# The experts' down products as three fp32r ones, with weight parts by half units

## The reference, cut to what matters

```
hid = silu(einsum('td,edf->etf', t, w_gate)) * einsum('td,edf->etf', t, w_up)   # 1024 -> 512
hid = hid * combine.T[:, :, None]        # two experts of sixteen for each token
y = einsum('etf,efd->td', hid, w_down)   # 512 -> 1024
```

## Time and profile before

| | us |
|---|---|
| median of 3 runs | 2130.91 |
| lowest and highest | 2128.61, 2133.64 |
| the profiled execution | 2131.86 |
| its span (first to last instruction) | 2130.3 |
| the experts' rounds in it, from the first slot rows asked for to the last down's end | 588.1 to 951.9 |

### The profile page before, as it was taken

How to read it: one execution, slowest core, us unless ns; L and a number is a source line. 1 busy time by engine, 2 the same in 40 slices (tenths; PEclk the granted TensorE clock), 3 DMA queues, 4 the chain that set the end, 5 groups by cost and what they waited for, 6 DMA issues and landing times.

```text
span 2130.3 us, 22099 instructions
## 1 busy us (share of the span) xinstructions
PE 1841.3 (86%) x8371; PEld 1407.6 (66%) x8371; DVE 849.6 (40%) x1337; ACT 775.0 (36%) x1222; POOL 280.7 (13%) x380
## 2 busy tenths in 40 slices
PE   5995999999469998975999999697777859999996
PEld 4883666668346666644888888585463648888885
DVE  3545334434435555545332332623443262323324
ACT  3224554542234444433222222322546232213221
POOL 2100432220100000001000000513406100000000
PEclk9997999999689999996999999897779879999998
DMA  5226523124369999674332332323010022323321
GB/s 179 87 82 216 197 76 116 57 83 168 150 231 341 345 337 343 226 248 154 93 98 89 110 91 87 102 89 104 1 40 1 30 70 79 99 89 99 99 99 50
DMA packets 182126, 279.69 MB, mean 131 GB/s; under 512 B 9554, under 2 KB 135073, under 8 KB 169616
## 3 DMA queue, kind: packets, MB, share of 16 engines
q1 hardware_dynamic: 170000, 244.36, 34.8%
q0 software_dynamic: 12032, 34.06, 4.7%
HBM read 241.13 MB, written 35.16 MB: 130 GB/s over the span
## 4 chain that ended last, share of the span: by engine, by line
PE 78%; DVE 8%; DMA 5%; ACT 3%; issue 3%; POOL 2%; SPq 0%; POOLq 0%; DVEq 0%; ACTq 0%
PE psum L402 21%; PE psum L403 20%; PE psum L404 20%; PE psum L1143 5%; PE psum L538 3%; PE psum L556 3%; PE psum L527 2%; DMA arena<-x_slots 2%; DVE warea_r L373 2%; POOL arena L645 2%; DMA warea<-in_w_in 1%; ACT warea_r L366 1%; DVE tarea_r L1655 1%; PE psum L1112 1%; DVE harea L1627 1%
## 5 line engine op out<-in xcount | busy, mean ns | idle before, releaser
L393 DVE TENSOR_TENSOR warea_r<-warea,warea_r 128x2048 fp32r<-128x2048 f32 x114 | 266.6, 2339 | 411.2 <-ACT warea_r L387 411.1
L402 PE MATMUL psum<-tarea_r,warea_r 128*128 128x512 f32 x896 | 357.4, 399 | 12.6 <-DVE tarea_r L1655 12.6
L403 PE MATMUL psum<-tarea_r,warea_r 128*128 128x512 f32 x896 | 351.9, 393 | 0.0
L404 PE MATMUL psum<-tarea_r,warea_r 128*128 128x512 f32 x896 | 351.5, 392 | 0.0
L387 ACT ACTIVATE warea_r<-warea 128x2048 fp32r<-128x2048 f32 x114 | 217.7, 1911 | 289.7 <-PE psum L404 281.3
L402 PE MATMUL psum<-warea_r,arena_r 128*128 128x512 f32 (+1 forms) x640 | 251.2, 392 | 34.5 <-DVE warea_r L373 31.0
L404 PE MATMUL psum<-warea_r,arena_r 128*128 128x512 f32 (+1 forms) x640 | 247.0, 386 | 0.0
L403 PE MATMUL psum<-warea_r,arena_r 128*128 128x512 f32 (+1 forms) x640 | 246.8, 386 | 0.0
L402 PEld LDWEIGHTS psum<-tarea_r,warea_r 128*128 128x128 f32 x896 | 170.1, 190 | 53.6 <-DVE tarea_r L1655 13.3
L404 PEld LDWEIGHTS psum<-tarea_r,warea_r 128*128 128x128 f32 x896 | 170.1, 190 | 36.3
L403 PEld LDWEIGHTS psum<-tarea_r,warea_r 128*128 128x128 f32 x896 | 170.2, 190 | 33.6
(11 more groups left out here) (290 smaller groups left out, 2405.7 us busy)
## 6 DMA issues: line engine op xcount, KB each, us to landing
warea<-in_ffn_w_gu SPq DMA_DIRECT2D x88, 512.0 KB, 5.0
warea<-in_w_in SPq DMA_DIRECT2D x48, 512.0 KB, 4.7
warea<-in_ffn_w_down SPq DMA_DIRECT2D x40, 512.0 KB, 4.2
arena<-in_w_up SPq DMA_DIRECT2D x16, 1024.0 KB, 6.5
tarea<-in_w_up SPq DMA_DIRECT2D x16, 1024.0 KB, 6.8
tarea<-in_w_down SPq DMA_DIRECT2D x16, 1024.0 KB, 5.6
warea<-in_w_gate SPq DMA_DIRECT2D x14, 1024.0 KB, 8.8
harea<-in_w_gate SPq DMA_DIRECT2D x14, 1024.0 KB, 8.2
```

The costliest lines, as they stand in the source:

```text
L393: dve.tensor_tensor(w_lo[:, u % 2, :], raw[:, u % RAW, :], w_hi[:, u % 2, :].bitcast(f32), ALU.subtract)\
L402: nc.tensor.matmul(out, high, by_high, start=first, stop=False)
L403: nc.tensor.matmul(out, high, by_low, start=False, stop=False)
L404: return nc.tensor.matmul(out, low, by_high, start=False, stop=last)
```

## The change

- The hidden features are split in `HT_hi` (ScalarE) and `HT_lo` (VectorE), and a down product is three fp32r ones, which read `w_hi` and `w_lo`. So the down units go through `moe_high` and `moe_low` as well, in the order of the units.
- A part is made, waited for and released by halves of a unit, 1024 columns: `moe_hi`, `moe_lo` and `moe_done` count halves.
- A place of the ring of raw weights is free when its low part exists (`moe_lo`), no longer when its matmuls are through.
- The queues of ScalarE and VectorE get the down units' parts: ScalarE after the silu, VectorE partly before `hb` and partly after it. `HT_lo` stands before `y_copy`.
- Before the last down, TensorE reads no register any more.

The diff, cut to its core:

```diff
-    HTs = carve(5120, 4, P)
+    HT_hi, HT_lo = part(A_AT + 5120, 4, P), part(A_AT + 5632, 4, P)
...
     def moe_high(b, i):
...
         act.wait_ge(moe_in[slot], 16 * fills)
-        if i >= 2:
-            act.wait_ge(s["moe_done"], n - 1)
-        elif not isinstance(b, int) or b >= 1:
-            act.wait_ge(s["moe_done"], n - 3 if not isinstance(b, int) or b >= 2 else i + 3)
-        act.activation(w_hi[:, parity, :], moe_raw[slot], ACT.Copy).then_inc(s["moe_hi"], 1)
+        for h in range(2):
+            at = ds(1024 * h, 1024)
+            if not (isinstance(n, int) and n < 2):
+                act.wait_ge(s["moe_done"], 2 * (n - 2) + (h + 1))
+            act.activation(w_hi[:, parity, at], moe_raw[slot][:, at], ACT.Copy).then_inc(s["moe_hi"], 1)
 
     def moe_low(b, i):
...
-        dve.wait_ge(s["moe_hi"], 4 * b + (i + 1))
-        dve.tensor_tensor(w_lo[:, parity, :], moe_raw[slot], w_hi[:, parity, :].bitcast(f32), ALU.subtract)\
-            .then_inc(s["moe_lo"], 1)
+        for h in range(2):
+            at = ds(1024 * h, 1024)
+            dve.wait_ge(s["moe_hi"], 2 * n + (h + 1))
+            dve.tensor_tensor(w_lo[:, parity, at], moe_raw[slot][:, at], w_hi[:, parity, at].bitcast(f32), ALU.subtract)\
+                .then_inc(s["moe_lo"], 1)
...
                 if isinstance(n, int) and n >= 12 and b < STATIC:
-                    sp.wait_ge(s["moe_done"], n - 11)
+                    sp.wait_ge(s["moe_lo"], 2 * (n - 11))
                 elif not isinstance(n, int):
-                    sp.wait_ge(s["moe_done"], n - 5)
+                    sp.wait_ge(s["moe_lo"], 2 * (n - 5))
...
             def gate_up(b):
                 pe.wait_ge(s["xt_low"], 2 * b + 2)
                 for i in range(4):
-                    pe.wait_ge(s["moe_lo"], 4 * b + (i + 1))
+                    n = moe_unit(b, i)[0]
                     for k in range(4):
-                        c = 4 * (i % 2) + k
+                        c, h = 4 * (i % 2) + k, k // 2
+                        if k % 2 == 0:
+                            pe.wait_ge(s["moe_lo"], 2 * n + (h + 1))
...
-                    mm.then_inc(s["moe_done"], 1)
+                        if k % 2:
+                            mm.then_inc(s["moe_done"], 1)
...
-                pe.wait_ge(s["hts_ready"], b + 1)
+                pe.wait_ge(s["hts_low"], b + 1)
...
                 for i in range(2):
-                    n, slot, fills = moe_unit(b + 1, first_unit + i)
-                    pe.wait_ge(moe_in[slot], 16 * (filled if filled is not None else fills))
+                    n = moe_unit(b + 1, first_unit + i)[0]
                     for c in (2 * i, 2 * i + 1):
+                        pe.wait_ge(s["moe_lo"], 2 * n + (c % 2 + 1))
                         for hf in range(2):
                             at = 1024 * (c % 2) + 512 * hf
-                            mm = nc.tensor.matmul(ps[4 + hf], HTs[:, c, :], moe_raw[slot][:, at:at + 512], start=c == 0, stop=c == 3)
-                    mm.then_inc(s["moe_done"], 1)
+                            mm = products(ps[4 + hf], HT_hi[:, c, :], HT_lo[:, c, :], w_hi[:, i % 2, at:at + 512],
+                                          w_lo[:, i % 2, at:at + 512], c == 0, c == 3)
+                        mm.then_inc(s["moe_done"], 1)
...
                 nc.scalar.activation(sg, ps[0], ACT.Silu).then_inc(s["silu_done"], 1)
+                if not zero:
+                    moe_high(b, 4)
+                    moe_high(b, 5)
                 slot_high(b + 1)
-                for i in range(2):
-                    moe_high(b + 1, i)
+                moe_high(b, 4 if zero else 6)
+                moe_high(b, 5 if zero else 7)
                 act.wait_ge(s["htr_psum"], b + 1)
-                nc.scalar.activation(HTs, ps[6].rearrange("p (c q) -> p c q", c=4), ACT.Copy).then_inc(s["hts_ready"], 1)
+                nc.scalar.activation(HT_hi, ps[6].rearrange("p (c q) -> p c q", c=4), ACT.Copy).then_inc(s["hts_ready"], 1)
...
-                for i in (2, 3):
+                for i in (2, 3, 4):
                     moe_low(b, i)
                 dve.wait_ge(s["silu_done"], b + 1)
-                dve.wait_ge(s["moe_done"], n0 + 4)
+                dve.wait_ge(s["moe_done"], 2 * n0 + 8)
                 V.tensor_tensor(hb, ps[1], sg, ALU.mult).then_inc(s["hb_ready"], 1)
+                if not zero:
+                    moe_low(b, 5)
                 slot_low(b + 1)
-                for i in range(2):
-                    moe_low(b + 1, i)
                 if not zero:
-                    y_copy(b - 1, n0 + 6)
+                    moe_low(b, 6)
+                moe_low(b, 5 if zero else 7)
+                dve.wait_ge(s["hts_ready"], b + 1)
+                V.tensor_tensor(HT_lo, ps[6].rearrange("p (c q) -> p c q", c=4), HT_hi.bitcast(f32), ALU.subtract)\
+                    .then_inc(s["hts_low"], 1)
+                if not zero:
+                    y_copy(b - 1, 2 * n0 + 12)
```

More of the change, by code:

```diff
@@ L330, in build_blocks @@
         route_psum chosen exp_in exp_out slots_ready routed zero_ready zero_out scattered x_slot xtr_psum xt_ready xt_low
-        silu_done hb_ready htr_psum hts_ready yb_ready yb_high y_out y_back0 y_back1 y_back2 y_back3 y_used
+        silu_done hb_ready htr_psum hts_ready hts_low yb_ready yb_high y_out y_back0 y_back1 y_back2 y_back3 y_used
         ff_silu gated hid_high ff_hid fd_psum f_evac
@@ L768, in _ @@
                 n, slot, _ = moe_unit(last + 1, i)
-                sp.wait_ge(s["moe_done"], 6 * last + i)
+                sp.wait_ge(s["moe_lo"], 12 * last + 2 * i)
                 src = w["w_down"][0][ds(final, 1), :, :].rearrange("o (p c) f -> p (o c) f", p=P)
@@ L791, in ffn_half @@
                     feed(u0 + v)
-            sp.wait_ge(s["moe_done"], 78)
+            sp.wait_ge(s["moe_lo"], 156)
             ffn_half(0, "ffn1", AT_FFN1)
@@ L1129, in hidden_features, with down @@
                 mm.then_inc(s["htr_psum"], 1)
-            def down(b, first_unit, filled=None):
-                pe.wait_ge(s["hts_ready"], b + 1)
+            def down(b, first_unit):
+                pe.wait_ge(s["hts_low"], b + 1)
                 if not (isinstance(b, int) and b == 0):
@@ L1160, in _ @@
                 expert_round(b)
-            filled = pe.value_load(isml[0:1, 33:34], min_val=STATIC - 6, max_val=NSLOT_BLOCKS - 7)
-            down(last, 0, filled)
+            down(last, 0)
             pe.wait_ge(s["yb_ready"], last + 1)
@@ L1479, in expert_round @@
                 moe_high(b, 3)
-                act.wait_ge(s["moe_done"], n0 + 2)
+                act.wait_ge(s["moe_done"], 2 * n0 + 4)
                 if not zero:
@@ L1483, in expert_round @@
                 nc.scalar.activation(sg, ps[0], ACT.Silu).then_inc(s["silu_done"], 1)
+                if not zero:
+                    moe_high(b, 4)
+                    moe_high(b, 5)
                 slot_high(b + 1)
-                for i in range(2):
-                    moe_high(b + 1, i)
+                moe_high(b, 4 if zero else 6)
+                moe_high(b, 5 if zero else 7)
                 act.wait_ge(s["htr_psum"], b + 1)
-                nc.scalar.activation(HTs, ps[6].rearrange("p (c q) -> p c q", c=4), ACT.Copy).then_inc(s["hts_ready"], 1)
+                nc.scalar.activation(HT_hi, ps[6].rearrange("p (c q) -> p c q", c=4), ACT.Copy).then_inc(s["hts_ready"], 1)
                 if not zero:
-                    y_high(b - 1, n0 + 6)
+                    y_high(b - 1, 2 * n0 + 12)
             act.wait_ge(s["mix_psum"], 8)
@@ L1501, in _ @@
                 expert_round(b)
-            y_high(last, moe_unit(last + 1, 1)[0] + 1)
+            y_high(last, 2 * moe_unit(last + 1, 1)[0] + 2)
             split_high(AT_FFN1)
@@ L1925, in _ @@
             V.tensor_scalar(isml[:, 32:33], off[:, 15:16], float(STATIC), None, ALU.add)
-            V.tensor_scalar(isml[:, 33:34], off[:, 15:16], float(STATIC - 6), None, ALU.add)
             V.tensor_copy(isml[:, 8:18], eb).then_inc(s["routed"], 1)
@@ L1961, in _ @@
                 expert_round(b)
-            y_copy(last, moe_unit(last + 1, 1)[0] + 1)
+            y_copy(last, 2 * moe_unit(last + 1, 1)[0] + 2)
             dve.wait_ge(s["y_out"], 16 * last + 16)
```

## The result

The changed kernel takes 2141.13 us, median of 8 runs (2136.41 to 2148.37), against 2128.62 of the kernel before beside it (8 runs). The ratio is 1.0052, interval 1.0036 to 1.0068 (the medians alone give 1.0059): slower by half a per cent. The forecast was 2128, a little faster; the time lies in the range of 2109 to 2143, but near its end and on the other side of no change. The profiled execution has a span of 2139.3, against 2130.3; the share of TensorE in the chain went from 78% to 73%.

A forecast was written before the change was run, and what follows sets the result against it. TensorE's round (21.15 us) and the slot-row load behind the y store were taken to bound the experts' stage nearly equally. Terms -1.7 - 5.8 - 0.9 + 6.0 = -2.4 on 2131.9, less 1.0, gave 2128; range 2109 to 2143.

The forecast's parts named there:

- the last three rounds: Final rounds of the experts' stage, S13 to S16: put at 18.1, 18.5 and 20.7 us, a predicted difference of -6.5.
- L: Time from issuing the load of slot rows to its landing; median 9.4 us in eleven rounds, 5.3 to 8.2 in the last three.
- the start: First two rounds of the experts' stage: holes, a shorter wait and no half clock gain 6.8 us, less 1.0 allowed: -5.8.
- the tail: From the start of down(14) to the end of the last down: 15.8 us become 14.9, so -0.9.
- The new period: One experts' round: max(18.1, 12.5 + L) us, with rows asked for 12.5 us after the slot transposes start.
- VectorE's 18.0 us a round: VectorE's work per experts' round: 18.0 us, fitting barely, and itself the bound if periods fell to 18.1.
- L keeps its values: Load of slot rows in the experts' stage: old trip times kept, eleven at the median 9.4 us; rounds sum to -1.7.
- a sign of being wrong: The prediction called itself wrong if, among other signs, the trip of slot rows left 8.5 to 10.6 us.
- The +1.0 set aside for the first load: At the start, 2 MB more weights queue beside the first load of rows: +1.0 us allowed, from nothing up to 2.0.
- The clock: TensorE idling 3.8 us before slot transposes: half clock in four of eleven rounds, about 1.5 each, +6.0; bounds 0 and 16.5.
- Rival 2: Clock falls in most rounds: ten falls in place of four give 2137 us, with L at 10.0 2144; chance 0.20.
- Rival 1: Trip of slot rows gets shorter, so the DMAs bound at 365 GB/s, 20.1 us a round: 2109; chance 0.17.

The follow-up runs named there:

- experiment 1: Changed kernel with the load of slot rows issued ahead of the store of y on GpSimd's queue: 2076.23 us, ratio 0.9744 to the kernel before.
- experiment 2: Changed kernel with both y copies moved ahead of the last half unit and the hidden features, GpSimd's order kept: 2105.82 us, ratio 0.9883 to the kernel before.
- experiment 9: Changed kernel with places of raw weights released by `moe_done`, after the matmuls, instead of `moe_lo`: 2138.44 us, ratio 1.0034 to the kernel before.
- Experiment 5: Changed kernel with VectorE making the next unit 0's low part after `hb` and the slot's low part in round 0: 2133.73 us, ratio 1.0029.
- experiment 6: Kernel before with only the half units for gate and up, the down product left as one fp32 matmul: 2117.39 us, ratio 0.9942.
- experiment 7: Kernel before with only the half units, plus the load of slot rows issued ahead of the store of y: 2090.98 us, ratio 0.9813.
- experiment 8: Changed kernel with early load of rows, mended VectorE order in round 0 and three filler matmuls before the last down: 2069.74 us, ratio 0.9717.
- experiment 3: Changed kernel with two unused fp32 matmuls between the gate and up products and the wait for rows: 2132.47 us, ratio 1.0024 to the kernel before.
- the repeat: The changed kernel itself, run again unchanged on the same chip: 2142.30 us, ratio 1.0051 to the kernel before.

## Why the prediction went wrong

The mechanism, rows asked for behind a later y copy, was right. The sign was wrong, and the steps that failed are three terms outside the steady rounds: the last three rounds, above all their L (8.8 us too low), the start (3.9) and the tail (4.4). The eleven steady rounds were put 4.8 us too long, which hid a part of this, and the parts that the change doesn't touch came out 0.9 shorter: together the 11.4 us between the -2.4 that was said and the +9.0 of the spans. That the time still lies in the range owes something to this cancelling.

**The new period.** Right. The step said 12.5 + L; it measured 12.0 + L where the clock was full, and 13.6 + L where it had fallen. Eleven periods are 11 x 12.0 + 6 x 1.6 + 99.5 of trips (mean 9.05) + 0.5 between landings and transposes + 0.4 for a first load asked for at 12.35 = 242.0, against 242.1. The step was 0.5 too high in the offset and 0.35 in L, the clock 3.6 too low over all; so the near agreement is in part luck. Experiments 1 and 2 show cause and place: asked for early, the whole of it goes. VectorE's 18.0 us a round, with which it might have been the bound, measured 17.0 in experiment 1.

**L keeps its values.** Nearly right for the steady rounds: 8.0 to 10.1 against 7.8 to 10.6, though four trips of 8.0 to 8.2 lie below the 8.5 that the prediction had named as a sign of being wrong. For the last three rounds it failed, and this is the largest error, 8.8 us: I took 5.3, 6.0 and 8.2 over the earlier trace rows, and they were 3.9, 12.0 and 10.2. The two long trips are 8.0 of it; most of the rest is a fall of the clock at 912.6, which put the last load at S + 14.0 and had no price there. Those are the rounds in which SP's queue starts again after its pause, with six units in 15 us. Its first pair goes out at 897.9, ahead of the store and load at 902 and 903, where before it went out with them (903.7), and the weights of the feed-forward block come beside the load at 929. I had read the old trips as a property of the stage; most likely they were one of when each queue fires, for which experiment 9 speaks in part (9.35 and 8.93 with the later release).

**The start.** -5.8 was said, -1.9 came. The two holes go. But I took the wait of 4.23 us as one for unit 4's parts alone, and did not ask what is queued behind the low part that VectorE had been given before `hb`. It measured 4.67, and half clock followed. Experiment 5 gives 3.4 of the missing 3.9. There the wait is the 2.3 that I had worked out, but the 1.5 for the clock was wrong even so: it fell behind 2.31 us, in experiments 5 to 8 alike. The +1.0 set aside for the first load was too much, and made up for half of that: 8.87 against 8.59. The Trainium skill ("DMA: Bandwidth & Descriptors", Queues, rings and completion order) has each DMA engine take turns between queues; the traces agree: the first load took 8.6 to 9.0 us in the five profiles without the 2 MB more beside it, and 8.7 to 8.9 in the seven with them.

**The tail.** -0.9 was said, +3.5 came. Of the 4.4 between them 4.2 are half clock: 1.6 in the round after S16, and 2.6 in the last down, which waited 3.29 us for the y copy (9.4 us from copy to copy, 6.8 in experiment 8 with its fillers). I had put a price on the clock in eleven rounds and forgot it here.

**The clock.** Four falls of eleven at 1.5 were said, six at 1.6 came in the first profile and more in the second; experiment 3 gives 9.9 us for those of the steady rounds. Rival 2 said 2137 to 2144 by this mechanism, and the time is in there; but in the profile it is only a part of it, beside the last rounds, the start and the tail. The Trainium skill ("TensorE: Matmul & The Clock Gate", Part 1) warns of loops that wait for a DMA each time round; the trace agrees, with six of eleven rounds.

**Rival 1** was worked out with a bound that does not hold, 365 GB/s. The sum didn't use it, only the lower end of the range, 2109, which moreover kept the 6.0 us for the clock though rounds of 20.1 would leave 2.0 us idle. It hid how much lay in the y path: with it I put a round at 20.1, and it is 17.76.

## What to carry to other kernels

When a change shortens the engine that sets the time, write down for each queue when it asks for the next input, counted from the same event in the round. Here that moved by half a microsecond to two the wrong way, because the copy that frees the queue stood last in a queue that had got more to do. A load whose own condition was met ten microseconds ago should not stand behind a store that waits; moving it was worth 65 us. With this or with the y copies first (35 us) the change paid; with the edits of experiments 3, 5 and 9 alone it didn't.

A stretch of the trace with fewer transfers tells the length of a trip only for that order of issues; take it as a bound, not as a term.

## What the runs showed of the hardware

A DMA share of 0.94 was not the end of what the DMAs could do, and could not be scaled up: 343 GB/s at 0.94 would give 365 at a full share, and experiment 1 moved 407 to 422 at 1.00 to 1.02, in ten rounds one after another.

The length of an idle piece alone does not say whether TensorE's clock falls. In the changed kernel it fell from 2.4 to 1.2 GHz at pieces of 2.04, 3.46, 3.51, 3.80, 4.10 and 4.32 us, and stayed through 3.27 and 3.39. In the repeat it fell at 1.91 and 3.08 and stayed through 3.27. In experiment 6 it fell behind pieces of 1.85 and 1.90.
